# Dilated attention with its sequence sorted by residues: near scores of 32 queries against 256 keys on column quarters, one 512-column score tile a unit, four transposes

## The reference, cut to what matters

```python
u = h @ w_in
q, k, v, gate = jnp.split(u, [QKV_DIM, 2 * QKV_DIM, 3 * QKV_DIM], axis=-1)
q = partial_rope(rms_norm(q.reshape(shp), q_norm), cos, sin)
k = partial_rope(rms_norm(k.reshape(shp), k_norm), cos, sin)
...
for g, (window, dilation) in enumerate(DILATION_GROUPS):
    # query t attends keys t - j*dilation for j = 0..window/dilation
    o, lse = dilated_band_attention(q[:, :, g], k[:, :, g], v[:, :, g], dilation, window // dilation)
    outs.append(o)
    lses.append(lse)
wts = jax.nn.softmax(jnp.stack(lses, axis=0), axis=0)
o = jnp.sum(wts[..., None] * jnp.stack(outs, axis=0), axis=0)
y = o.reshape(B, S, ATTN_OUT_DIM) * jax.nn.silu(gate)
return y @ w_out
```

## Time and profile before

| | |
|---|---|
| median of 3 runs | 1907.56 us (1906.88 to 1907.57) |
| the profiled execution | 1906.24 us |
| its span, first to last instruction | 1904.4 us |
| TensorE matmuls busy | 1848.3 us, 97% of the span |
| TensorE weight loads busy | 1455.6 us, 76% |
| ScalarE busy | 1133.2 us, 60% |
| VectorE busy | 918.4 us, 48% |
| stage 4 in the trace | about 339 us to 686 us |

### The profile page before, as it was taken

One profiled execution on the slowest core, in us unless ns is written; L12 is line 12 of the kernel. 1 busy time (PEld: TensorE's weight loads), 2 busy tenths in 40 slices (PEclk: granted clock), 3 DMA queues, 4 the chain that ended last, 5 costly groups with the idle time before them and its releaser, 6 DMA issues.

```text
span 1904.4 us, 23279 instructions
## 1 busy us (share of the span) xinstructions
PE 1848.3 (97%) x8370; PEld 1455.6 (76%) x8370; DVE 918.4 (48%) x1683; ACT 1133.2 (60%) x1506; POOL 305.5 (16%) x396
## 2 busy tenths in 40 slices
PE   5999799999999989999999999999998999999999
PEld 3888478777777767888888886667766888888887
DVE  3899766657576756322221145597555432222100
ACT  5675667656566556755554457666564665555533
POOL 0111011322222101111111111001110111111111
PEclk8999899999999899999999999999999999999999
DMA  6988488865555347888889987545653778888897
GB/s 191 223 203 214 115 218 196 207 163 124 136 121 134 91 111 189 198 188 192 197 194 220 237 204 170 122 107 133 159 131 82 196 191 197 194 191 195 206 212 191
DMA packets 93972, 330.55 MB, mean 174 GB/s; under 512 B 12352, under 2 KB 12608, under 8 KB 93248
## 3 DMA queue, kind: packets, MB, share of 16 engines
q0 software_dynamic: 45696, 156.79, 44.4%
q1 hardware_dynamic: 44640, 160.19, 25.7%
q10 hardware_dynamic: 3552, 12.44, 1.8%
HBM read 166.32 MB, written 6.29 MB: 91 GB/s over the span
## 4 chain that ended last, share of the span: by engine, by line
PE 82%; DVE 11%; ACT 3%; issue 2%; DMA 2%; ACTq 0%; DVEq 0%
PE ps L1620 70%; DVE cv_acc L1168 4%; PE ps L1637 2%; PE ps L1672 2%; PE ps L1816 1%; PE ps L1859 1%; PE ps L1828 1%; PE ps L1845 1%; DMA X<-x 1%; DMA w_lo<-w_raw 1%; PE ps L2073 1%; DVE ds_P L1412 0%; ACT w_hi L474 0%; PE ps L1978 0%; PE ps L2134 0%
## 5 line engine op out<-in xcount | busy, mean ns | idle before, releaser
L1620 PE MATMUL ps<-H_hi,w_hi 128*128 128x512 f32 x1272 | 508.5, 400 | 5.6 <-DMA w_lo<-w_raw 4.8
L1620 PE MATMUL ps<-H_hi,w_lo 128*128 128x512 f32 x1272 | 495.5, 390 | 0.0
L1620 PE MATMUL ps<-H_lo,w_hi 128*128 128x512 f32 x1272 | 495.2, 389 | 0.0
L439 POOL DMA_DIRECT2D w_lo<-w_raw x296 | 256.9, 868 | 1461.5 <-ACT w_lo L484 1437.3
L474 ACT ACTIVATE w_hi<-w_raw 128x1024 fp32r<-128x1024 f32 x299 | 313.7, 1049 | 120.1 <-PE ps L1620 119.5
L484 ACT ACTIVATE w_lo<-w_raw 128x1024 fp32r<-128x1024 f32 x299 | 311.9, 1043 | 0.0
L1620 PEld LDWEIGHTS ps<-H_hi,w_hi 128*128 128x128 f32 x1272 | 238.8, 188 | 65.0 <-issue 12.3
L1620 PEld LDWEIGHTS ps<-H_lo,w_hi 128*128 128x128 f32 x1272 | 238.8, 188 | 55.2 <-issue 6.7
L1620 PEld LDWEIGHTS ps<-H_hi,w_lo 128*128 128x128 f32 x1272 | 238.7, 188 | 50.3
L1041 DVE SCALAR_TENSOR_TENSOR X<-ps,X 128x512 f32<-128x512 f32 (+1 forms) x36 | 27.0, 751 | 251.6 <-PE ps L1620 244.0
L1620 PE MATMUL ps<-mid_hi,w_hi 128*128 128x512 f32 x352 | 136.9, 389 | 0.0
(11 more groups left out here) (344 smaller groups left out, 2734.8 us busy)
## 6 DMA issues: line engine op xcount, KB each, us to landing
w_raw<-weights SPq DMA_DIRECT2D x299, 512.0 KB, 4.6
w_lo<-w_raw POOLq DMA_DIRECT2D x296, 512.0 KB, 5.4
X<-x ACTq DMA_DIRECT2D x4, 512.0 KB, 12.7
pl_P<-spill ACTq DMA_DIRECT2D x1, 2048.0 KB, 7.8
spill<-X ACTq DMA_DIRECT2D x8, 256.0 KB, 5.2
X<-spill ACTq DMA_DIRECT2D x2, 1024.0 KB, 5.6
out<-X SPq DMA_DIRECT2D x8, 256.0 KB, 5.8
at_pair<-at_raw POOLq DMA_DIRECT2D x96, 16.0 KB, 1.9
```

The source lines that it names most:

```text
L439: pool.dma_start(w_lo[:, u, :], w_raw[:, u, :], accum_op=ALU.add).then_inc(lo_landed[u], 16)
L1620: mm = pe.matmul(ps[:, bank, :], w, x, start=first and n == 0 and q == 0, stop=last and n == len(blocks) - 1 and q == 2, skip_group_check= ...
```

## The change

- The columns of `H_hi` and `H_lo` that stage 3 writes for stage 4 are put in residue order: column 128 r + l is position 4 l + r. The positions for the angles, the sum of squares of the input (`x_totalled`) and the masks follow it. `gate` reads its gate in this order.
- A unit's 128 queries, and the keys of its residue, are then neighbouring columns; before, they were every fourth column.
- Near scores: the 128 queries of a unit are taken as four blocks b of 32, and each block is multiplied with its own 256 keys (32 of each residue, of the block before and of its own) instead of all 512. Block b is written to partitions 32 b to 32 b + 31, that is, computed on a quarter of the array's columns. Block 0 has no block before it and is multiplied twice with its own 128 keys.
- Far scores are computed in the same four quarters, since all scores of a unit now lie in one bank: 256 near columns, then 128 and 128.
- VectorE reduces the 512 columns of a unit at once, behind the step that makes its far scores; the separate near reduction, its semaphore `near_done` and the maximum over both are gone. The exponential and the scaling are 512 columns wide.
- Four transposes in place of six; they alternate between banks 4 and 5, and the wait of every other unit for `pt_done` is gone. Scores alternate between banks 2 and 3 (the last chunk: 2, 3, 0, 1), and a step waits for `m_done` of the unit before last.
- The values of group 0 are written by VectorE in an order that fits the turned probabilities, in runs of 32.

```diff
+WINDOW = 2 * P
+QB = P // NQ
...
-            return at_Sm[:, (u % 3 if a == 3 else u % 2), :]
+        def unit_home(u):
+            return at_Sm[:, u % 2, :]
...
+        def score_bank(a, u):
+            return (2, 3, 0, 1)[u % 4] if a == 3 else 2 + u % 2
+
+        def turned_bank(u):
+            return 4 + u % 2
...
-                        act.activation(hi[:, j, :], X[:, j, :], ACT.Copy, scale=col(gain, j)).then_inc(split_hi, 1)
+                        dst, src = hi[:, j, :], X[:, j, :]
+                        if order is not None:
+                            dst, src = residues(dst), order(src)
+                        act.activation(dst, src, ACT.Copy, scale=col(gain, j)).then_inc(split_hi, 1)
...
-                        if u >= 0:
-                            st, probs = at_st[:, u % 4, :], unit_home(a, u)
-                            link(dve.tensor_tensor_reduce(
-                                out=probs[:, S:S + 2 * P], in0=ps[:, far_bank(a, u), 0:2 * P], in1=at_far[:, :],
-                                scale=HEAD ** -0.5, scalar=TAKEN, op0=ALU.add, op1=ALU.max, accum_out=st[:, 3:4]))
-                            dve.wait_ge(near_done, UNITS * a + u + 1)
-                            link(dve.tensor_tensor(st[:, 0:1], st[:, 0:1], st[:, 3:4], ALU.max))
-                            dve.tensor_scalar(st[:, 1:2], st[:, 0:1], -1.0, None, ALU.mult).then_inc(m_done, 1)
-                        if j < UNITS:
-                            dve.tensor_tensor_reduce(
-                                out=unit_home(a, j)[:, 0:S], in0=ps[:, near_bank(a, j), :], in1=at_near[:, j // 2, :],
-                                scale=HEAD ** -0.5, scalar=TAKEN, op0=ALU.add, op1=ALU.max,
-                                accum_out=at_st[:, j % 4, 0:1]).then_inc(near_done, 1)
+                        st = at_st[:, u % 4, :]
+                        link(dve.tensor_tensor_reduce(
+                            out=unit_home(u), in0=ps[:, score_bank(a, u), :], in1=at_mask[:, unit_rows(u)[1], :],
+                            scale=HEAD ** -0.5, scalar=TAKEN, op0=ALU.add, op1=ALU.max, accum_out=st[:, 0:1]))
+                        dve.tensor_scalar(st[:, 1:2], st[:, 0:1], -1.0, None, ALU.mult).then_inc(m_done, 1)
...
+            def near_scores(a, u, b):
+
+                rows, r = unit_rows(u)
+                q = 6 * (a % 2)
+                out = ps[QB * b:QB * (b + 1), score_bank(a, u), 0:WINDOW].rearrange("p (j r l) -> p j r l", j=2, r=4)
+                keys = residues(at_raw[rows, q + 1, :])
+                queries = at_raw[rows, q, r * P + QB * b:r * P + QB * (b + 1)]
+                if b:
+                    window = keys[:, :, QB * (b - 1):QB * (b + 1)].rearrange("p r (j l) -> p j r l", j=2)
+                    return pe.matmul(out, queries, window, start=True, stop=True)
+                return [pe.matmul(out[:, j], queries, keys[:, :, 0:QB], start=True, stop=True) for j in (1, 0)][-1]
+
+            def far_scores(a, u, g, b):
+
+                rows, r = unit_rows(u)
+                q = 6 * (a % 2) + 2 * g
+                at = WINDOW + (g - 1) * P
+                return pe.matmul(ps[QB * b:QB * (b + 1), score_bank(a, u), at:at + P],
+                                 at_raw[rows, q, r * P + QB * b:r * P + QB * (b + 1)],
+                                 at_raw[rows, q + 1, r * P:(r + 1) * P], start=True, stop=True)
...
-                    mm = pe.matmul(ps[:, near_bank(a, near), :], at_raw[rows, q, r:S:4], at_raw[rows, q + 1, :],
-                                   start=True, stop=True)
...
+                for b in (3, 2, 1, 0):
+                    if far is not None:
+                        mm = far_scores(a, far, 1, b)
+                    if near is not None and b:
+                        near_scores(a, near, b)
+                if far is not None:
+                    for b in (3, 2, 1, 0):
+                        mm = far_scores(a, far, 2, b)
+                if near is not None:
+                    mm = near_scores(a, near, 0)
                 mm.then_inc(s_done, 1)
...
-                if u % 2:
-                    pe.wait_ge(pt_done, UNITS * a + u)
-                for b in range(6):
-                    mm = pe.transpose(ps[:, 4 + b // 4, (b % 4) * P:(b % 4 + 1) * P], probs[:, b * P:(b + 1) * P], ident)
+                probs = unit_home(u)
+                for n, b in enumerate((1, 0, 2, 3)):
+                    mm = pe.transpose(ps[:, turned_bank(u), n * P:(n + 1) * P], probs[:, b * P:(b + 1) * P], ident)
```

More of the change, by code:

```diff
@@ L525, in square_x, with new_x @@
                 k.up(x_summed)
-            def new_x(m, n, hi, gain, made):
+            def new_x(m, n, hi, gain, made, order=None):
                 act.wait_ge(made, k.up(made))
@@ L545, in norm, with ple @@
                     split(H_hi[:, c, :], c % 2)
-            def ple(hi, gain):
+            def ple(hi, gain, order=None):
                 prep()
@@ L557, in ple @@
                         prep()
-                    new_x(u, 1, hi, gain, x_new)
+                    new_x(u, 1, hi, gain, x_new, order)
             def adds_to_x(parts, hi, gain, squared=True, between=None, keep=False):
@@ L1028, in sum_x, with split_x @@
                 dve.wait_ge(x_summed, k.up(x_summed))
-            def split_x(m, n, hi, lo, gain):
+            def split_x(m, n, hi, lo, gain, order=None):
                 if hi is not None:
@@ L1062, in normed, with ple @@
                         between[c]()
-            def ple(pl_P, hi, lo, gain):
+            def ple(pl_P, hi, lo, gain, order=None):
                 prep()
@@ L1076, in ple @@
                     if u:
-                        split_x(u - 1, 1, hi, lo, gain)
+                        split_x(u - 1, 1, hi, lo, gain, order)
                     dve.wait_ge(gated, k.up(gated))
@@ L1818, in step_scores @@
-                if far is not None:
-                    rows, r = unit_rows(far)
-                    if far == 0:
-                        pe.wait_ge(n_done, normed + len(QK_TILES) * (a + 1))
-                    if a == 3 and far == 1:
+                    elif a == 3 and near == 3:
                         pe.wait_ge(v_copied, GROUPS * 4)
                         pe.wait_ge(var_done, 4 * len(QK_TILES))
-                    elif UNITS * a + far:
-                        pe.wait_ge(m_done, UNITS * a + far - (a == 3 and far > 1))
-                    for g in (1, 2):
-                        mm = pe.matmul(ps[:, far_bank(a, far), (g - 1) * P:g * P], at_raw[rows, q + 2 * g, r:S:4],
-                                       at_raw[rows, q + 2 * g + 1, r:S:4], start=True, stop=True)
+                    elif UNITS * a + near > 1:
+                        pe.wait_ge(m_done, UNITS * a + near - (3 if a == 3 and near > 3 else 1))
```

94 lines of the change are left out of this document (49 added, 45 removed).

## The result

The changed kernel takes **1888.08 us** (median of 5 runs, 1887.7 to 1888.53); the kernel before, beside it, 1906.93 (1905.86 to 1907.57). The ratio is 0.990, 95% interval 0.9888 to 0.9911: 18.9 us faster, 1.0%. The profiled execution took 1887.96, with a span of 1886.2 against 1904.4. The forecast was 1888.7. The sum agrees, but four of its terms do not, and the rest of this text is about them.

The account below looks back on a forecast made before the run. TensorE, busy 97% of the span, was taken to set the pace, with a chain of waits in the last chunk. The terms sum to -18.9 us: profiled 1906.24 becomes 1887.3, the median 1.3 above, 1888.7; range 1883 to 1899.

Parts of the forecast that it names:

- transposes: TensorE, 24 units of the first three chunks: two transposes of 0.11 us less in each, -5.3 us.
- combined steps, 21: Steps with near and far scores on TensorE: 0.96 us in place of 1.32, in 21 steps -7.6 us.
- near-only, far-only: Steps with only near or only far scores, three of each: 0.72 us each, -1.7 and -1.8 us.
- value transposes: Contiguous weight loads of the value transposes may give 0.01 us in 32 of them: -0.3 us.
- VectorE's waits: TensorE waits for VectorE's scaling ahead of units 2, 3 and 7: three times 0.7, +2.1 us.
- last chunk: Stage 4's last chunk, a chain of waits: -5.0 us, the least certain term, from -1 to -7.
- stage 3 to 4: ScalarE and VectorE read every fourth column for the last block at stage 3's end: +0.7 us (0 to 1.2).
- The lower bound given, 0.70: A combined step with everything side by side: 0.44 + 0.26 = 0.70 us.
- rival of two tiles at once: Only two column tiles stream at once: a combined step of 1.14 us, the kernel at 1895.5; chance 0.17.
- that of no overlap: Column quarters do not overlap at all: a combined step of 2.02 us, the kernel at 1920.6; chance 0.06.
- rival of a least cost of 62 ns: Each score pass costs at least 0.062 us: a combined step of 1.87 us, the kernel at 1910.4; chance 0.10.
- The clock rival: TensorE's clock stays low, at 1.2 GHz, in the last chunk: +5, the kernel at 1893.7 us; chance 0.09.

Follow-up runs that it names:

- e_six_turns: The changed kernel with six transposes a unit again, two of them doing the near half a second time: 1889.39 us.
- e_by_quarter: The changed kernel with the same score matmuls issued quarter by quarter, both far ones and then the near one for each block: 1888.19 us.
- e_max_early: The changed kernel with VectorE's maximum and negation a slot earlier, ahead of the rotation, in the first three chunks: 1884.36 us.
- e_totals_in_order: The changed kernel with the matmul that totals the squares reading its columns in order again, VectorE reordering the result: 1886.47 us.

## Why the prediction was right, and where it was not

| term | forecast | shown |
|---|---|---|
| transposes | -5.3 | -5.2 |
| combined steps, 21 | -7.6 | -12.8 |
| near-only, far-only | -3.5 | -3.8 |
| value transposes | -0.3 | -0.3, by starts, not tested by itself |
| VectorE's waits | +2.1 | +4.2 |
| last chunk | -5.0 | -5.5 |
| stage 3 to 4 | +0.7 | +2.2 |
| clock elsewhere | none | about +3 |
| sum | -18.9 | -18.2 of the profiled span |

The forecast of the total came true; one argument in it, on the order of the scores, failed. It mis-sized the combined steps and, through them, VectorE's waits; the term for stage 3 to 4 was mis-sized by itself.

*Transposes*: right; four passes 0.109 us apart. e_six_turns puts 0.22 a unit back and only some of the units pay, as the waits would have it.

*Combined steps*: "block 0's near scores stand behind four far matmuls that can only start once the first far ones are through" is the step that failed. In its place stands a step of 0.62 where it was 1.23, 0.61 saved and not 0.36, or 0.72 us with the change-over where 0.96 was forecast; e_by_quarter shows that the order of these 26 passes is free. The lower bound given, 0.70, was the truth, nearly. The Trainium skill's rule (TensorE: Matmul & The Clock Gate, "Measured speedup vs the span model"), starts some 4 ns apart, gave the estimate of 0.75 and -12.0 and was nearer than mine; the trace has 7 ns. Full overlap of quarters, the base of the forecast, held. The rival of two tiles at once (1.14) and that of no overlap fell. The rival of a least cost of 62 ns fell too: the 26 passes start within 0.43 us. My argument against it was faulty, though: at 0.043 us a pass the sum that it uses gives 1.12 + 0.26 = 1.38, longer than 1.32, and not "a step 1.2 at worst, still shorter". What the forecast did not have is that 64x32 tiles did not overlap with 64x128 ones; the change happened to quarter both kinds of scores, and half of it would have ended 20 us slower than the kernel before.

*VectorE's waits*: the chain was right, 7.91 forecast and 7.92 measured. The waits are twice as large because TensorE, the other side of the difference, got faster than I had it: 7.19 for a unit in place of 7.44 gives 0.73 at unit 3 in place of 0.47, and 0.35 and 0.33 in place of 0.2 at units 2 and 7. So this error follows from the one before and returned 2.1 of its 5 us. It is no law of the kernel, though: e_max_early takes all of it away.

*Last chunk*: within 0.5 of the forecast, though called the least certain. Its parts by starts: up to the first transposes 638.71 - 635.02 = 3.69 us where it was 4.99, so 1.3 saved; units 0 to 3 2.7; units 3 to 7 1.3; forecast 1.4, 2.3 and 1.3. No experiment parted them. The clock rival did not come: the granted clock is 0.84 there, it was 0.81.

*Stage 3 to 4*: mis-sized, +0.7 in place of 1.27 + 0.94 = 2.2. The wait of 0.86 from which it started is the weight loads'; the matmuls' own is 0.43. The two reads came to +0.48 and +0.40 where I had 0.3 and 0.4, but "the seven blocks ahead of it lie under TensorE's tiles" failed for the next-to-last, whose `H_lo`, 0.38 longer, stands in VectorE's queue ahead of the last block's work (335.36 above). And the totals matmul, +0.94, was in the diff and in none of my terms: a strided moving side cost TensorE double (0.88 us a pass against 0.43). e_totals_in_order takes that part back exactly.

*Clock elsewhere*: from 252 to 262 us the granted clock is 0.83 where it was 1.00, and the same matmuls lose 1.6 us; 1.4 more are lost behind 686 us. The change touches neither place.

*What made it come out right*: the steps gave 5.5 more than forecast, and 2.1 in waits, 1.5 in stage 3 to 4 and about 3 in clock levels took it away again. That these cancel to 0.6 us is luck. By its terms the range was earned, the 0.6 us of distance was not.

## What to carry to other kernels

When matmuls use part of the array, give everything that should run together one tile width; the mixed form can be slower than no tiling at all. The order within a group of such matmuls needed no care up to 26 passes (more were not tried in another order), the strides do: a strided stationary side (328 ns against 188) and a strided moving side (0.88 us against 0.43 for a pass of 512 columns) both cost TensorE time, and here a reordering cost nothing once it was put on VectorE, which waits. After a gain on the bounding engine, look at which engine ends its new waits and at what that engine itself stands waiting for: here a reduction moved past four independent operations gave back 3.7 us for nothing.

## What the runs showed of the hardware beyond what I expected

- Tiles of 64 rows by 32 columns: eight at once, first passes 7 ns apart, and a later matmul for a free tile starts ahead of earlier ones whose tile is busy (L1826 at 499.25, 12 far passes after it).
- Tiles of 64x128 and 64x32 on different rows did not overlap: 1.94 us in four turns, 1.21 in two, 0.62 with one shape.
- Of 52 passes of such tiles, the first 31 start 16 ns apart on the mean, the other 21 some 30 ns; why they slow down is open. A weight load of 32 columns takes 102 to 107 ns.
- A read of every fourth fp32 column: ScalarE 1.20 us against 0.725, VectorE 1.15 against 0.753, TensorE's moving side 0.88 against 0.43 a pass of 512. VectorE's product in runs of 32 columns costs nothing: 0.692.
- After the same DMA wait of 3.0 to 3.4 us (between 686 and 716 us, by kernel), the next 0 to 13 passes or so of TensorE ran at 1.2 GHz, another number in each profiled execution: up to some 2.7 us between them.
